# A hybrid decoder step on one core: the sample group's probability-value products in fp32r, with the values split into a rounded part and a remainder

## The reference

```
def cross_attn(h, mem_k, mem_v, w_xq, w_xo):
    q = (h @ w_xq).reshape(b, L, X_HEADS, X_HEAD_DIM)          # 4 heads of 256
    s = jnp.einsum('blhd,bmhd->bhlm', q, mem_k) * (X_HEAD_DIM ** -0.5)
    pr = jax.nn.softmax(s, axis=-1)
    o = jnp.einsum('bhlm,bmhd->blhd', pr, mem_v).reshape(b, L, D_MODEL)
    return o.astype(h.dtype) @ w_xo
```

## Time and profile before

| | |
|---|---|
| median of 3 runs | 1327.97 us (1327.3 to 1332.85) |
| the profiled execution | 1328.24 us, of which the span from first to last instruction is 1326.5 us |
| busy, share of the span | PE 95%, DVE 57%, ACT 34%, POOL 12% |
| mean granted clock of TensorE | 0.978 of full speed |
| line 1908, the products changed here | 128 instructions between 823.6 and 884.5 us |

### The profile page before, as it was taken

How to read it: one execution, slowest core, us unless ns; L and a number is a source line. 1 busy time by engine, 2 the same in 40 slices (tenths; PEclk the granted TensorE clock), 3 DMA queues, 4 the chain that set the end, 5 groups by cost and what they waited for, 6 DMA issues and landing times.

```text
span 1326.5 us, 23554 instructions
## 1 busy us (share of the span) xinstructions
PE 1266.1 (95%) x9799; PEld 1190.4 (90%) x9799; DVE 760.0 (57%) x1494; ACT 451.2 (34%) x752; POOL 163.9 (12%) x194
## 2 busy tenths in 40 slices
PE   6999999999998999699999998999999999999996
PEld 5999998998887988699999985459999999999996
DVE  5677866666776656753444457323645765743433
ACT  4444423333332235432245223223431331322422
POOL 1000003000112733200010000001112222200000
PEclk7999999999998999899999997999999999999998
DMA  6423222222124563042234639401645556433211
GB/s 220 120 64 94 73 65 82 73 65 64 33 80 130 144 163 93 32 161 96 88 104 168 214 108 366 161 0 64 206 138 179 176 178 190 144 112 96 96 64 65
DMA packets 141701, 158.15 MB, mean 119 GB/s; under 512 B 4506, under 2 KB 132682, under 8 KB 141169
## 3 DMA queue, kind: packets, MB, share of 16 engines
q1 hardware_dynamic: 135764, 135.37, 32.8%
q0 software_dynamic: 4384, 21.15, 4.8%
q10 hardware_dynamic: 1456, 0.23, 0.1%
HBM read 140.70 MB, written 16.70 MB: 119 GB/s over the span
## 4 chain that ended last, share of the span: by engine, by line
PE 88%; DVE 6%; ACT 2%; issue 1%; DMA 1%; POOL 1%; SPq 0%; DVEq 0%; ACTq 0%
PE slot L376 70%; PE slot L1908 2%; PE slot L1819 2%; PE aux L1667 2%; DVE junk L1412 1%; PE aux L1660 1%; PE aux L1661 1%; PE aux L1881 1%; PE slot L1899 1%; DMA vr<-in_conv_b 1%; DMA w_raw<-in_w_xo 1%; DVE w_lo L361 1%; ACT w_hi L354 1%; PE aux L1644 1%; PE aux L1646 1%
## 5 line engine op out<-in xcount | busy, mean ns | idle before, releaser
L361 DVE TENSOR_TENSOR w_lo<-w_raw,w_hi 128x1024 fp32r<-128x1024 f32 x186 | 249.8, 1343 | 351.7 <-ACT w_hi L354 351.5
L354 ACT ACTIVATE w_hi<-w_raw 128x1024 fp32r<-128x1024 f32 x186 | 196.9, 1059 | 555.8 <-PE slot L376 519.6
L376 PE MATMUL slot<-a_hi,w_hi 128*128 128x260 f32 x1408 | 296.0, 292 | 0.7 <-DVE a_lo L1453 0.7
L376 PE MATMUL slot<-a_hi,w_lo 128*128 128x260 f32 x1408 | 284.5, 284 | 0.0
L376 PE MATMUL slot<-a_lo,w_hi 128*128 128x260 f32 x1408 | 283.9, 283 | 0.0
L376 PEld LDWEIGHTS slot<-a_hi,w_hi 128*128 128x128 f32 x1408 | 221.2, 190 | 12.8 <-issue 9.7
L376 PEld LDWEIGHTS slot<-a_lo,w_hi 128*128 128x128 f32 x1408 | 218.2, 189 | 0.0
L376 PEld LDWEIGHTS slot<-a_hi,w_lo 128*128 128x128 f32 x1408 | 217.9, 189 | 0.0
L376 PE MATMUL slot<-b_hi,w_hi 128*128 128x260 f32 x640 | 129.0, 283 | 1.6 <-DVE gate_b L1281 1.6
L376 PE MATMUL slot<-c_hi,w_hi 128*128 128x260 f32 x640 | 129.4, 283 | 0.2 <-DVE c_lo L1365 0.2
L376 PE MATMUL slot<-b_hi,w_lo 128*128 128x260 f32 x640 | 129.0, 283 | 0.0
(11 more groups left out here) (402 smaller groups left out, 1596.2 us busy)
## 6 DMA issues: line engine op xcount, KB each, us to landing
w_raw<-in_w_in SPq DMA_DIRECT2D x32, 1024.0 KB, 6.1
w_raw<-in_w_up SPq DMA_DIRECT2D x16, 1024.0 KB, 5.4
w_raw<-in_w_down SPq DMA_DIRECT2D x16, 1024.0 KB, 5.2
sring<-in_state_ssm SPq DMA_DIRECT2D x16, 512.0 KB, 5.4
w_raw<-in_w_ssd_proj SPq DMA_DIRECT2D x8, 1024.0 KB, 5.1
cache<-in_cache_mem_k SPq DMA_DIRECT2D x8, 1024.0 KB, 7.8
cache<-in_cache_mem_v SPq DMA_DIRECT2D x8, 1024.0 KB, 5.0
uring<-in_state_ssm SPq DMA_DIRECT2D x16, 512.0 KB, 4.0
```

The lines of the kernel that those rows point to most:

```text
L354: nc.scalar.activation(w_hi[:, t % 2], w_raw[:, t // 2 % 2, :, t % 2 * P:t % 2 * P + P], ACT.Copy).then_inc(hi_ready, 1)
L361: nc.vector.tensor_tensor(w_lo[:, t % 2], w_raw[:, t // 2 % 2, :, t % 2 * P:t % 2 * P + P], w_hi[:, t % 2].bitcast(F32), ALU.subtract).the ...
L376: last = nc.tensor.matmul(slot[t % 2][:, h, 0:HALF], w[:, t % 2, k, :], act[:, k, h * HALF:(h + 1) * HALF], start=(start and k == 0 and n ...
```

## The change

The 16 loop halves of `values_s` read, in place of the raw values in plain float32, their rounded part (`cache_hi`, a ring of 4 new half-block buffers) and their remainder (`cache_lo`, written in place over the raw block) in fp32r. For each head two matmuls are issued, one for each part. The weights are now 16 columns: 8 for the rounded part of the probabilities and 8 for their remainder. PSUM gathers 16 rows, and the two sets of 8 are added when they are turned, by a matmul with `pick` (which holds for each of 8 columns a one in two rows) in place of the transpose.

The split is done by ScalarE (`value_split`) and VectorE (`value_rest`), two halves ahead of the loop and then one in each step n, for the half n+2. `p_diag` is filled with two copies and two subtractions in place of 16 copies. Two semaphores elsewhere are merged into others (`dtw_lo_s` into `consts`, `fin_sum` into `fin_sq`), with no instruction added or moved there.

```diff
-        p_diag = at("p_diag", [P, 2, NS, XH, NS], R_4 + 8192)
-        o_tok = at("o_tok", [NS, D], R_4 + 10240)
+        PW = 2 * NS
+        p_diag = at("p_diag", [P, 2, NS * (XH * PW + 1)], R_4 + 8192, R32)
+        o_tok = at("o_tok", [2 * NS, D], R_4 + 12416)
+        cache_lo = [at(f"cache_lo{k}", [P, 2, D], R_1 + 8192 * k, R32) for k in range(CR)]
+        cache_hi = [at(f"cache_hi{k}", [P, D], (R_4, R_4 + 4096, g, g + 4096)[k], R32) for k in range(4)]
...
+            def value_split(n):
+                b, m = n // 2, n % 2
+                c = NS + b
+                if m == 0:
+                    act.wait_ge(cache_in[c % CR], 16 * (c // CR + 1))
+                    if b >= 2:
+                        act.wait_ge(cache_used, NS + b - 1)
+                nc.scalar.activation(cache_hi[n % 4][:], cache[c % CR][:, m, :], ACT.Copy).then_inc(value_hi, 1)
+
             act.wait_ge(sm_b, 1)
             nc.scalar.activation(prob_s[:], slot[0][0:32, 1, 0:MEM], ACT.Exp, bias=stats[0:32, 1:2], scale=XD ** -0.5,
                                  accum_out=stats[0:32, 2:3]).then_inc(sm_c, 1)
+            value_split(0)
+            value_split(1)
...
+                if n < 14:
+                    value_split(n + 2)
                 if n == 14:
                     act.wait_ge(cache_used, 2 * NS)
                     for j in range(2):
-                        nc.scalar.activation(o_tok[:, j * 512:(j + 1) * 512], slot[j][0:NS, 1, :], ACT.Copy).then_inc(o_s_row, 1)
+                        nc.scalar.activation(o_tok[:, j * 512:(j + 1) * 512], slot[j][0:2 * NS, 1, :], ACT.Copy).then_inc(o_s_row, 1)
...
+            def own_columns(m, part):
+                return p_diag[:, m, :].rearrange("p (b s) -> p b s", b=NS)[:, :, part * NS:XH * PW:PW]
+
+            probs = slot[1][:, 1, 0:64].rearrange("p (m b h) -> p m b h", m=2, b=NS)
             for m in range(2):
-                for b in range(NS):
-                    ins = nc.vector.tensor_copy(p_diag[:, m, b, :, b], slot[1][:, 1, m * 32 + b * XH:m * 32 + (b + 1) * XH])
+                ins = nc.vector.tensor_copy(own_columns(m, 0), probs[:, m])
+            chain(ins)
+            for m in range(2):
+                ins = nc.vector.tensor_tensor(own_columns(m, 1), probs[:, m], own_columns(m, 0).bitcast(F32), ALU.subtract)
             ins.then_inc(sm_f, 1)
+
+            def value_rest(n):
+                c = NS + n // 2
+                dve.wait_ge(value_hi, n + 1)
+                nc.vector.tensor_tensor(cache_lo[c % CR][:, n % 2, :], cache[c % CR][:, n % 2, :], cache_hi[n % 4][:].bitcast(F32),
+                                        ALU.subtract).then_inc(value_lo, 1)
+
+            value_rest(0)
+            value_rest(1)
...
+                if n < 14:
+                    value_rest(n + 2)
...
             def values_s(b, m):
                 n = NS + b
-                pe.wait_ge(cache_in[n % CR], 16 * (n // CR + 1))
-                for h in range(XH):
-                    last = nc.tensor.matmul(slot[h // 2][0:NS, 1, h % 2 * XD:(h % 2 + 1) * XD], p_diag[:, m, b, h, :],
-                                            cache[n % CR][:, m, h * XD:(h + 1) * XD], start=(b == 0 and m == 0 and h % 2 == 0),
-                                            stop=(b == NS - 1 and m == 1 and h % 2 == 1), skip_group_check=True)
+                pe.wait_ge(value_lo, 2 * b + m + 1)
+                for part in range(2):
+                    for h in range(XH):
+                        cols_h = slice(h * XD, (h + 1) * XD)
+                        v = cache_lo[n % CR][:, m, cols_h] if part else cache_hi[(2 * b + m) % 4][:, cols_h]
+                        last = nc.tensor.matmul(slot[h // 2][0:2 * NS, 1, h % 2 * XD:(h % 2 + 1) * XD],
+                                                p_diag[:, m, (b * XH + h) * PW:(b * XH + h + 1) * PW], v,
+                                                start=(b == 0 and m == 0 and part == 0 and h % 2 == 0),
+                                                stop=(b == NS - 1 and m == 1 and part == 1 and h % 2 == 1), skip_group_check=True)
...
-                        last = nc.tensor.transpose(slot[0][:, 1, k * NS:(k + 1) * NS], o_tok[:, k * P:(k + 1) * P], ident[0:NS, 0:NS])
+                        last = nc.tensor.matmul(slot[0][:, 1, k * NS:(k + 1) * NS], o_tok[:, k * P:(k + 1) * P],
+                                                pick[0:2 * NS, :].bitcast(F32), start=True, stop=True)
```

More of the change, by code:

```diff
@@ L277, in build @@
         spilled, reloaded = sem("spilled"), sem("reloaded")
-        dtw_hi_s, dtw_lo_s, dt_mm, dt_evac = (sem(n) for n in ("dtw_hi_s", "dtw_lo_s", "dt_mm", "dt_evac"))
+        dtw_hi_s, dt_mm, dt_evac = (sem(n) for n in ("dtw_hi_s", "dt_mm", "dt_evac"))
         dt_a, dt_b, dt_tr, cs_mm, cs_v = (sem(n) for n in ("dt_a", "dt_b", "dt_tr", "cs_mm", "cs_v"))
@@ L303, in build @@
         cache_used = sem("cache_used")
+        value_hi, value_lo = sem("value_hi"), sem("value_lo")
         q_split, qt_mm, qt_ev, qb_mm = (sem(n) for n in ("q_split", "qt_mm", "qt_ev", "qb_mm"))
@@ L309, in build @@
         ff_sq, ff_hi, ff_lo = (sem(n) for n in ("ff_sq", "ff_hi", "ff_lo"))
-        gain_in, fin_mm, fin_copy, fin_sq, fin_sum, fin_std, fin_ev = (
-            sem(n) for n in ("gain_in", "fin_mm", "fin_copy", "fin_sq", "fin_sum", "fin_std", "fin_ev"))
+        gain_in, fin_mm, fin_copy, fin_sq, fin_std, fin_ev = (
+            sem(n) for n in ("gain_in", "fin_mm", "fin_copy", "fin_sq", "fin_std", "fin_ev"))
         D_ORDER = (0, 1, 4, 2, 5, 3, 6, 7)
@@ L598, in _ @@
             pool.wait_ge(gemm_done, T_XO)
-            nc.gpsimd.memset(p_diag[:], 0.0).then_inc(p_zero, 1)
+            nc.gpsimd.memset(p_diag[:].bitcast(F32), 0.0).then_inc(p_zero, 1)
             pool.wait_ge(kt_ev, 4)
@@ L951, in _ @@
             ins.then_inc(fin_sq, 1)
-            act.wait_ge(fin_sum, 1)
+            act.wait_ge(fin_sq, 2)
             nc.scalar.activation(stats[:, 16:20], stats[:, 12:16], ACT.Sqrt, bias=eps_col[:, 0:1], scale=1.0 / D).then_inc(fin_std, 1)
@@ L1013, in _ @@
                     dve.wait_ge(dtw_hi_s, 1)
-                    nc.vector.tensor_tensor(dtw_lo[:], dtw[:], dtw_hi[:].bitcast(F32), ALU.subtract).then_inc(dtw_lo_s, 1)
+                    nc.vector.tensor_tensor(dtw_lo[:], dtw[:], dtw_hi[:].bitcast(F32), ALU.subtract).then_inc(consts, 1)
             u_lo(6)
@@ L1504, in _ @@
             dve.wait_ge(fin_sq, 1)
-            nc.vector.tensor_tensor(stats[:, 12:16], stats[:, 0:4], stats[:, 4:8], ALU.add).then_inc(fin_sum, 1)
+            nc.vector.tensor_tensor(stats[:, 12:16], stats[:, 0:4], stats[:, 4:8], ALU.add).then_inc(fin_sq, 1)
             dve.wait_ge(fin_std, 1)
@@ L1561, in residual_norm @@
                 norm_tile(q, KT - 1, False, True)
-            pe.wait_ge(dtw_lo_s, 1)
+            pe.wait_ge(consts, 6)
             for k in range(KT):
```

## The result

| | before | changed |
|---|---|---|
| median | 1330.41 us (4 runs, 1327.3 to 1336.03) | 1348.48 us (4 runs, 1348.21 to 1352.81) |
| profiled execution, span | 1326.5 | 1351.1 |
| mean granted clock | 0.978 | 0.963 |

The changed kernel is slower by 1.3%: ratio 1.0131, 95% interval 1.0105 to 1.0156. Forecast were 1340 us, within 1335 to 1352.

A forecast was written before the change was run, and what follows sets the result against it. TensorE alone was taken to bound the loop before, a ring of waits after. Steps +13.8, start +0.4 and end -2.3 made the stage 11.9 us longer: 1328.24 became 1340.1 us, range 1335 to 1352.

The forecast's parts named there:

- The ring: Attention loop: closed waits through VectorE, TensorE and ScalarE, with rounding and remainder in them; step 4.06 us against 3.05.
- The first rival: Loop: new work hides behind the matmuls, TensorE still bounds, step 2.19 us, time 1314.4; chance 0.05.
- The second rival: Loop: rounding and remainder take only 0.60 us each, closed waits 3.07 us, time 1326, no difference; chance 0.05.
- the ring at the high clock: Loop: step set by the closed waits, TensorE staying at 2.4 GHz; time 1338 to 1344, chance 0.72.
- the clock case: Loop and `w_xo`: TensorE falls to 1.2 GHz through idling; time 1345 to 1358, chance 0.18.
- start, to the first row maximum in the loop: Ahead of the loop: first splits and `p_diag` filling put the row maximum at 829.45 for 829.06, +0.4 us.
- thirteen steps: First to last row maximum in the loop: 10 × 4.06 + 3 × 8.48 = 66.0 us against 52.3, +13.8.
- step 14 to the end of its turn: Loop's end: products take 0.96 us, within the 1.56 to the turn's end, against 3.88 before; -2.3 us.
- from there to `w_xo`: Behind the loop: copy out, small matmuls and last turn as long as before, 0 us.
- `w_xo` to the end: Projection and after: nothing won back, 0 us in the sum; another 2 us if `w_xo` begins at 1.2 GHz.
- third rival: The clock falls within the loop: 1358 us for all of it, 1345 to 1352 for a part; chance 0.18.
- 59% of busy time: Loop: TensorE busy 2.4 of 4.06 us, held on the safe side of a clock fall, but not by much.

The follow-up runs named there:

- e1: Changed kernel with ScalarE's rounding of half n+2 moved right behind the exponential, ahead of the copy that waits for the turn; ratio to before 0.9963.
- e2: Changed kernel with VectorE's remainder made a step later, for half n+1 in step n; ratio to before 1.0021.
- e3: Kernel before, plain float32 products kept, with rounding and remainder added unused at the changed kernel's places; ratio to before 1.0110.
- e8: e3 with the rounding right behind the exponential and the remainder ahead of the subtractions that wait for `values(h)`; 1332.43 us, one run.
- e9: e6 with VectorE's row maximum of step n+1 moved behind the scaling of step n; 1319.41 us, ratio to before 0.9915.
- e4: Changed kernel with 8 more fp32r matmuls, results unread, behind the products in steps 2 to 13; ratio to before 1.0110.
- e7: Kernel before with the 8 transposes of `o_tok` made plain float32 matmuls with the same identity; ratio to before 1.0019.
- e6: e5 with the outputs turned by 8 transposes again and VectorE adding the two sets of 8; ratio to before 0.9943.
- e5: e1 with VectorE's remainder put ahead of the two subtractions in steps 3, 7 and 11; 1320.44 us, one run.

## Why the prediction came out as it did

**The ring** was right in its place, its members and its size: 4.10 us for 4.06, with 1.89 us of idling on VectorE (forecast 1.86 from the same sum) and 1.87 on TensorE. e1 opens it, e2 shortens it, e3 keeps it and e8 leaves it, and the step follows each time. The first rival, that the work hides behind the matmuls and the step falls to 2.19, is what e1 (2.47) in part and e9 (2.11) in full make true by moving instructions. In the changed kernel it was false, for the reason that the prediction gave. The second rival fell with the rows 1.05 and 1.23: a rounding and a remainder of values are as long as those of weights.

**The size** was 7.5 us short: +11.9 forecast, +19.4 measured (17.3 in the stage, 2.1 behind it; +18.1 by the medians). The median of 1348.48 us lies within 1335 to 1352 but outside the 1338 to 1344 that the prediction gave to the ring at the high clock. It is in the range because the range took in a part of the clock case, and two of the terms that filled the distance, the turn and `w_xo`, stand at 0 in the sum. The forecast also built on 1328.24 us, where the median of before became 1330.41. By the prediction's own terms, from the two traces:

| term | forecast | measured |
|---|---|---|
| start, to the first row maximum in the loop | +0.4 | +0.1 |
| thirteen steps | +13.8 | +17.4 |
| step 14 to the end of its turn | -2.3 | -1.9 |
| from there to `w_xo` | 0 | +1.7 |
| `w_xo` to the end | 0 | +2.1 |

- *Thirteen steps.* The ring gives 10 × 4.10 + 3 × 8.49 = 66.5 against 52.3, so +14.2. The other 3.2 are the low clock in two of the three steps with `values(h)`: 2.9 in the matmuls themselves (4.92 and 5.40 us for 3.70), 0.25 in the turn ahead of the first (0.69 for 0.44). e4 shows it: there they are gone. The ten other steps stayed at 4.10. The prediction kept this as its third rival with a chance of 0.18 and held 59% of busy time for safe, by stretches of 63% and 55% at the high clock. The step that failed is that comparison: a stretch that kept its clock doesn't show that its busy share always does. In the changed kernel's rows 2.13 and 2.22 of 4 us were followed by a fall and 2.24 was not, and over 834 to 904 us the clock was 0.86 where the prediction named 1.00 as a sign. The third rival is thus true in part. It was no case apart from the forecast but rode on it. Of the Trainium skill's rule on this ("TensorE: Matmul & The Clock Gate", section "A second HAM failure mode: psum-queue depth-cycling") the trace now has the case: gaps of 1.9 us, and a clock that goes down and up. The price in the loop was 3.2 us of the 16 that the full case would have had.
- *From the last turn to `w_xo`.* "As long as before" was wrong. The prediction looked at the copies and not at the form of the turn: a transpose is one instruction for each of 8 tiles, the float32 matmul with `pick` two, each with 128 columns of weights. e7 shows +1.3 us by itself, and e6 wins 1.4 back. The other 0.4 of the 1.7 is the clock: the 16 instructions took 1.95 us in e7 and e5, at 2.4 GHz, and 2.37 in the changed kernel, where the clock was 0.80 from 906.4 to 910.4 us.
- *`w_xo` to the end.* It starts at 1.2 GHz and needs over 5 us to be at 2.4 (0.64 us for two matmuls until 915.3, 0.40 from 915.7). The prediction priced this at 2 us, but only within its clock case. A low stretch at the start of `w_xo` or within about 1 us of it came in seven more kernels (e1 to e7), and not in e8 and e9. What decides it is open. In the kernel before, in e3 and in e8 TensorE's work ahead of `w_xo` is the same, 2.21 of the last 4 us busy at 2.4 GHz in each, and of these only e3 fell.

**The products** were costed at 0.96 us and their neighbours at 0.86 and 0.37; together 2.19. In e9 the three take 2.11 us from turn to turn, and its chain of waits has the products at 0.92 to 0.94, the scores at 0.86 and the turn at 0.31 to 0.33. The forecast gain was there, then, and no gain came of it as TensorE did not set the step.

## What to carry to other kernels

Here an instruction added to an in-order queue cost what it added to the rings of waits that run through its place, not its share of the engine's time (e3 against e8). Follow each ring from an instruction back to the same one a step later, through every queue and every wait, and put new work where its engine waits for somebody anyway: ahead of such a wait if its inputs are there. A ring that idles TensorE can cost once more through its clock. And if a float32 transpose becomes a matmul its instructions and its weight loads are counted anew.

## What the runs showed of the hardware that was not expected

- The same busy share gave both outcomes for TensorE's clock: with 2.1 to 2.2 of 4 us busy in the loop it stayed at 2.4 GHz after one stretch and fell to 1.2 GHz after others, within one execution; and three kernels with 2.21 of 4 us ahead of `w_xo` differ in whether it fell there. At 77% (e4, 52.69 of 68 us) it stayed up throughout.
- A float32 turn of an 8x128 tile took 0.08 us as a transpose (8 in 0.66) and 0.24 as a matmul with the same identity (16 instructions in 1.95).
- The eleven traces differ by up to 8 us ahead of the stage examined, in the same work (its start lies between 818.6 and 826.9 us), and the later starts have the lower granted clock (0.97 for 0.98). Two traces are compared by stage, not by their spans.
